# A fifth PSUM bank, decay rows stored by chunk, and decay factors by eight exponentials in the state-space stage of a two-block network

## The chip, the cores and the metric

The kernel runs on one core of one Trainium2 chip. The metric is the device time of that core in microseconds, the median of several executions. Everything is computed in float32; matrix products split each operand into a high part that TensorE takes in one pass and a low rest, and add three products.

## The reference

The reference is a network of two blocks over a sequence of 1024 tokens with 1024 features. The change touches one mixer of the second block, a Mamba-2 layer with 32 heads of width 64 in 4 groups of 8 heads, with a state of 128 per group, computed in 8 chunks of 128 tokens:

```
acum  = cumsum(dt * A)                       # within a chunk, per head
decay = exp(where(t >= s, acum[t] - acum[s], -inf))
y     = (C B^T * decay) @ (x * dt)  +  (C @ state) * exp(acum)
state = state * exp(acum[end])      +  B^T @ (x * dt * exp(acum[end] - acum))
y     = (y + D * x) * silu(z)
y     = rmsnorm over each group's 512 channels
out   = y @ w_out
```

Before that, `z`, `x`, `B` and `C` come from a projection of the normed input, and `x`, `B` and `C` go through a causal convolution of four taps and a silu. The rest of the network (gated spatial mixing, dilated attention, stick-breaking attention, two layers of per-layer embedding) is untouched.

## The kernel before

The activations are kept transposed: a tile holds 128 features on the partitions and 1024 tokens along the free dimension. All weight tiles (128x1024, 512 KB) lie in one array in the order of use. SP loads each into one of two raw buffers, ScalarE makes its high part (L114), and VectorE or GpSimd makes the low part (L119). A raw buffer is free for the tile after next when the low part is made; this is what SP waits for before each load.

`stage_dt` (L1177) computes the step sizes and the running sums: `acum` holds them by token (128 partitions, a column for each chunk and head), and `rows` by head. SP writes `rows` to memory as `acum_dram`, 32 heads by 1024 tokens.

`stage_ssm` (L1326) is a loop over the four groups of heads. In each group TensorE works in this order:

- six convolution tiles (two of B and C, four of x), each a dense product of 48 matmuls, half of them for each 512 columns, into the two banks of `D`;
- four z tiles, cut into 64 units of three matmuls. The first 20 units run alone, then come ten slots, in which units are mixed with the chunk work: `products(c)` (L1436 C times state, L1439 the state's increment, L1442 eight weighted products), `turn_out(c)` (L1450, transposes of y), `turn_in(c)` (L1429 to L1431, transposes of x and B, and the product C B). A slot holds `products` of one chunk, `turn_out` of the chunk before and `turn_in` of the chunk after next;
- sixteen output products of twelve matmuls each (eight row tiles, two halves), which use four banks in turn, number o in bank o % 4. The first four run over three of the four y tiles while the fourth is being made; then the sums of squares (L193), the root on ScalarE, the reciprocal on VectorE, the spread to all columns (L211), and VectorE's copy of it. Only then can VectorE scale an output product and add it to `f_sb` (L1717, L1720), and product o starts when the evacuation of product o - 4 has read its bank.

For each chunk the decay factors are made in `E`, two buffers of 128x1024 in `K.sq` (eight heads by 128 tokens). SP broadcasts the eight head rows to all partitions (L1391), GpSimd subtracts the token's own sum (L1743) and fills the upper triangle with -1e30 (L1746), ScalarE takes the exponential (L1546), and VectorE multiplies by C B (L1607), which releases L1442. A row for chunk c is issued when the products of chunk c - 2 are done. VectorE's other chunk work is x_dt and x_dte (L1599, L1601), the new state (L1615), the sum of y (L1619, L1622), the skip term (L1629), and the evacuation of z units (L1593).

SP's queue holds the loads of the group's weight tiles and the rows in a fixed order: `load(m)` waits for the low part of tile m of the group and fetches tile m + 2. Tiles 0 to 5 are the convolution's, 6 to 9 z's, 10 to 13 the output's. The order is `load(0)` to `load(5)`, rows 0 and 1, `load(6)`, rows 2 and 3, `load(7)`, and so on to `load(9)`, then `load(10)` to `load(13)`. Row 0 waits for the end of the last convolution.

Of the kernel before, what the change touches and what calls it, by code (L numbers as in the profile page):

```python
# [6 lines left out]
F32 = mybir.dt.float32  # L7
F32R = mybir.dt.float32r
ALU = mybir.AluOpType
ACT = mybir.ActivationFunctionType  # L10

P = 128
S = 1024
# [1163 lines left out]
def stage_dt(K, x_sb, f_sb, xhi, xlo, dt, dte, acum, e_acum, e_end, acum_dram):  # L1177
# [5 lines left out]
    with ExitStack() as ctx:  # L1183
# [23 lines left out]
        with nc.Block() as block:  # L1207
            @block.sync
            def _(sp):
                sp.dma_start(raw[:, :, :], io["w_dt"][:, :, :]).then_inc(landed, 16)  # L1210
                sp.dma_start(head[:, :, :], io["dt_head"][:, :].partition_broadcast(P)).then_inc(landed, 16)
                sp.dma_start(tri[:, :], io["causal"][:, :]).then_inc(landed, 16)
                sp.wait_ge(copied, 2)
                sp.dma_start(acum_dram, rows[:, :]).then_inc(stored, 16)
                sp.wait_ge(stored, 16)

            @block.tensor
# [56 lines left out]
            @block.vector  # L1274
            def _(dve):
                dve.wait_ge(h_done, 1)
                dve.tensor_tensor(lo[:, :, :], raw[:, :, :], hi[:, :, :].bitcast(F32), ALU.subtract).then_inc(l_done, 1)
                K.norm_recip(dve, root_done, rtok_done)
                K.norm_copy(dve, spread, spread_done, r_done)
                for k in range(KT + 1):  # L1280
                    if k < KT:
                        dve.scalar_tensor_tensor(f_sb[:, k, :], x_sb[:, k, :], K.gain("g_final", k), K.R[:, :],
                                                 ALU.mult, ALU.mult).then_inc(f_done, 1)
                    if k >= 1:
                        dve.wait_ge(f_done, k)
                        K.tile_lo(dve, xlo, xhi, f_sb, k - 1, "m_norm", x_hi, x_lo)
                dve.wait_ge(f_done, KT)
                K.norm_recip(dve, root2, rtok2)
                steps = [0]

                def step(ins):

                    steps[0] += 1
                    ins.then_inc(v_step, 1)
                    dve.wait_ge(v_step, steps[0])

                dve.wait_ge(t_step, 1)
                step(dve.tensor_tensor(by_head(v[:, :]), by_head(pN[:, 0:W]),
                                       K.rtok[:, :].unsqueeze(2).to_broadcast([P, NC, SH]), ALU.mult))
                dve.wait_ge(landed, 48)  # L1300
                step(dve.tensor_tensor(by_head(v[:, :]), by_head(v[:, :]), all_blocks(head[:, 0, :]), ALU.add))
                K.norm_copy(dve, spread, spread2, r2)


                dve.wait_ge(a_step, 4)
                step(dve.tensor_scalar(d[:, :], e[:, :], 1.0, None, ALU.add))
                step(dve.tensor_scalar(d[:, :], d[:, :], -1.0, 1e-30, ALU.add, ALU.add))
                step(dve.reciprocal(r[:, :], d[:, :]))
                step(dve.scalar_tensor_tensor(l[:, :], l[:, :], 1e-30, r[:, :], ALU.add, ALU.mult))
                step(dve.tensor_tensor(l[:, :], l[:, :], e[:, :], ALU.mult))  # L1310
                step(dve.scalar_tensor_tensor(dt[:, :], v[:, :], 0.0, l[:, :], ALU.max, ALU.add))
                step(dve.scalar_tensor_tensor(by_head(dA[:, :]), by_head(dt[:, :]), -1.0, all_blocks(expA[:, :]),
                                              ALU.mult, ALU.mult))
                dve.wait_ge(t_step, 3)
                step(dve.tensor_copy(acum[:, :], pA[:, 0:W]))
                step(dve.tensor_tensor(dte[:, :], pA[:, W:2 * W], acum[:, :], ALU.subtract))
                dve.tensor_copy(end[:, :], pA[:, W:2 * W]).then_inc(v_step, 1)
                dve.wait_ge(a_step, 6)
                dve.tensor_tensor(dte[:, :], dte[:, :], dt[:, :], ALU.mult)

            @block.gpsimd
            def _(pool):
# [3 lines left out]
def stage_ssm(K, xhi, xlo, f_sb, dt, dte, acum, e_acum, e_end, acum_dram):  # L1326
# [4 lines left out]
    with ExitStack() as ctx:  # L1331
# [5 lines left out]
        pY = ctx.enter_context(nc.psum_tensor("ssm_pY", [P, S], F32))  # L1337
        pS = ctx.enter_context(nc.psum_tensor("ssm_pS", [P, H], F32))
        pT = ctx.enter_context(nc.psum_tensor("ssm_pT", [P, H], F32))
        banks = [D[:, 0:H], D[:, H:S], pX[:, :], pT[:, :]]  # L1340
        BC = sb("BC", [P, 2, S])
        xs = sb("xs", [P, GT, S])
        with ExitStack() as shared:
# [14 lines left out]
        dn, evac = sem("dn"), sem("evac")  # L1358
        cv_a, cv_d, cv_s = sem("cv_a"), sem("cv_d"), sem("cv_s")
        row_land = [sem("row0"), sem("row1")]  # L1360
        seg, sel, ex, weighted, select_go = sem("seg"), sem("sel"), sem("ex"), sem("weighted"), sem("select_go")
        s1, ps_done, s2, s3, cb_copy, xd = sem("s1"), sem("ps"), sem("s2"), sem("s3"), sem("cb_copy"), sem("xd")
        y_inter, y_done, st_decay, st_done, y_turned = sem("y_inter"), sem("y_done"), sem("st_decay"), sem("st_done"), sem("y_turned")
        yz_early, y_hi_early, high_go = sem("yz_early"), sem("y_hi_early"), sem("high_go")
# [10 lines left out]
        with nc.Block() as block:  # L1375
            @block.sync
            def _(sp):
                def group(g):
                    def load(m):

                        n = GROUP_TILES * g + (n0 + m)
                        sp.wait_ge(K.w_lo, n + 1)
                        K.load_weight(sp, n + 2, m % 2)

                    def row(c):

                        if c == 0:
                            sp.wait_ge(cv_d, 18 * g + 18)
                        if c >= 2:
                            sp.wait_ge(s2, 8 * g + (c - 1))  # L1390
                        sp.dma_start(E[c % 2], acum_dram[bass.ds(8 * g, GH), c * P:c * P + P]  # L1391
                                     .partition_broadcast(P)).then_inc(row_land[c % 2], 16)

                    for m in range(6):
                        load(m)
                    for c in range(NC):
                        row(c)
                        if c % 2 == 1:
                            load(6 + c // 2)
                    for m in range(10, 14):  # L1400
                        load(m)

                with sp.Fori(0, GROUPS) as g:
                    group(g)

            @block.tensor
            def _(pe):
# [45 lines left out]
                def group(g):  # L1453
# [20 lines left out]

                    def out_products(o, k):
                        j, half = o // 2, o % 2
                        return K.products(pe, banks[o % 4], j // 2 % 2, 4 * (j % 2) + k, k, yhi, ylo, half,
                                          k == 0, k == GT - 1)


# [10 lines left out]
                    pe.wait_ge(y_lo, 4 * g + 4)  # L1491
                    for o in range(4):
                        out_products(o, GT - 1).then_inc(dn, 1)
                    pe.wait_ge(acc_done, 3 * g + 3)
                    K.norm_sums(pe, pCB, sums_done)
                    K.norm_spread(pe, pY, rtok_done, g + 1, spread_done)
                    for o in range(4, 2 * KT):
                        if o % 4 == 0:
                            pe.wait_ge(K.w_lo, GROUP_TILES * g + (n0 + 11 + o // 4))
                        pe.wait_ge(evac, OUTS * g + (20 + o - 1))  # L1500
                        for k in range(GT):
                            last = out_products(o, k)
                        last.then_inc(dn, 1)
# [5 lines left out]
            def _(act):  # L1509
# [9 lines left out]
                def group(g):  # L1519
# [17 lines left out]
                    for slot in range(10):  # L1537
                        if slot < 8:
                            c = slot
                            act.wait_ge(s1, 8 * g + (c + 1))  # L1540
                            if c >= 2:
                                act.wait_ge(s2, 8 * g + (c - 1))
                            act.activation(cb[:, c % 2, :, :], pCB[:, 0:2 * P].rearrange("p (a b) -> p a b", a=2),
                                           ACT.Copy).then_inc(cb_copy, 1)
                            act.wait_ge(sel, 8 * g + (c + 1))
                            act.activation(E[c % 2], E[c % 2], ACT.Exp).then_inc(ex, 1)  # L1546
                        q_old, q = q, q + sum(Z_UNITS[slot])
                        if q // 16 > q_old // 16:
                            silu_z(q // 16 - 1)
# [35 lines left out]
            def _(dve):  # L1585
# [48 lines left out]
                def group(g):  # L1634
# [78 lines left out]
                    for j in range(KT):  # L1713
                        for half in range(2):
                            cols = slice(half * H, half * H + H)
                            dve.wait_ge(dn, OUTS * g + (20 + 2 * j + half + 1))
                            dve.tensor_tensor(tmp[:, cols], banks[(2 * j + half) % 4], Rg[:, cols],  # L1717
                                              ALU.mult).then_inc(evac, 1)
                            dve.wait_ge(evac, OUTS * g + (20 + 2 * j + half + 3))
                            dve.tensor_tensor(f_sb[:, j, cols], f_sb[:, j, cols], tmp[:, cols], ALU.add).then_inc(scaled, 1)  # L1720
# [11 lines left out]
            def _(pool):  # L1732
                def group(g):
                    for c in range(NC):
# [5 lines left out]
                        for b in ([0, 1] if c == 0 else [c + 1] if c + 1 < NC else []):  # L1740

                            pool.wait_ge(row_land[b % 2], 64 * g + (16 * (b // 2) + 16))
                            pool.tensor_tensor(E[b % 2], E[b % 2], heads(acum, b, g, P), ALU.subtract).then_inc(seg, 1)  # L1743
                            pool.wait_ge(seg, 8 * g + (b + 1))
                            pool.sem_inc(select_go, 1)
                            pool.affine_select(out=E[b % 2], in_=E[b % 2], compare_op=ALU.is_ge, fill=NEG, base=0,  # L1746
                                               pattern=[[0, GH], [1, P]], channel_multiplier=-1).then_inc(sel, 1)
# [787 lines left out]
def bass_program(nc, io, out):  # L2535
    with ExitStack() as ctx:
# [5 lines left out]
        branch_a = nc.dram_tensor("branch_a", (KT, P, S), F32, kind="Internal").ap()  # L2542
        y_dram = nc.dram_tensor("y_b", (KT, P, S), F32, kind="Internal").ap()
        f_dram = nc.dram_tensor("f_copy", (P, KT, S), F32, kind="Internal").ap()
        acum_dram = nc.dram_tensor("acum_rows", (SH, S), F32, kind="Internal").ap()
        x_dram = io["xT"].rearrange("(k p) t -> p k t", p=P)

        ctx.callback(K.clear_semaphores)
# [114 lines left out]
```

## Time and profile before

| | |
|---|---|
| median of 3 runs | 3521.37 us (3518.78 to 3530.22) |
| the profiled execution | 3521.37 us |
| its span, first to last instruction | 3519.9 us |
| TensorE busy | 3181.3 us, 90% of the span |
| VectorE, ScalarE, GpSimd busy | 1852.6, 1359.8, 725.3 us |
| mean granted TensorE clock | 0.946 |
| the state-space stage | from 1486 to 2400 us of the span |

An engine's busy time says how long its instructions ran, not that they were needed at that moment. A row of the timeline has the start, the duration, the engine, the line, the operation with the tiles that it writes and reads, and in brackets the idle time before it with the engine and line that ended it. A granted clock of 1.00 is 2.4 GHz and 0.50 is 1.2 GHz.

### The profile page before, as it was taken

To read this page: it belongs to the slowest core of one execution; us is meant where nothing else is said; L and a number is where in the kernel's file an instruction comes from. 1 tells how busy PE (TensorE), PEld (TensorE's weight loads), DVE (VectorE), ACT (ScalarE), POOL (GpSimd) and SP (SyncE) were. 2 spreads that over 40 slices of the span, in tenths; PEclk is the share of its full clock that TensorE was granted. 3 is DMA by queue.
4 is the path that set the end of the run, shared out by engine and by line. 5 is a ranking of instruction groups with operands and counts; after the bars stand their busy time and mean duration, and the time that the engine had idled before them with its cause. 6 is when DMAs were issued, how large, how long until landed. Compare 5 with 4: busy or idle time off the path is not lost. (4 is left out here: it accounts for less than half of the span.)

```text
span 3519.9 us, 41749 instructions
## 1 busy us (share of the span) xinstructions
PE 3181.3 (90%) x15532; PEld 2634.1 (75%) x15532; DVE 1852.6 (53%) x2499; ACT 1359.8 (39%) x1876; POOL 725.3 (21%) x488
## 2 busy tenths in 40 slices
PE   7999999999997999588988989988889999998799
PEld 5788878888885777476766857767768888887677
DVE  4344215666665322556556555576346776766433
ACT  4333114555554312333222222233236666666331
POOL 2110002222221001202021030120224444443110
PEclk8999999999999999699999989999989999998899
DMA  2111221211211212012121131121111111111211
GB/s 93 44 49 44 77 78 54 61 55 55 67 55 42 102 66 96 21 42 66 42 52 51 42 73 35 48 56 60 61 54 37 37 37 37 37 41 44 108 66 60
DMA packets 83049, 197.35 MB, mean 56 GB/s; under 512 B 6304, under 2 KB 41760, under 8 KB 82624
## 3 DMA queue, kind: packets, MB, share of 16 engines
q1 hardware_dynamic: 74048, 164.66, 15.2%
q0 software_dynamic: 8832, 30.41, 2.8%
q8 instruction: 109, 1.79, 0.2%
q14 instruction: 60, 0.49, 0.0%
HBM read 165.56 MB, written 21.10 MB: 53 GB/s over the span
## 5 line engine op out<-in xcount | busy, mean ns | idle before, releaser
L114 ACT ACTIVATE whi<-wraw 128x1024 fp32r<-128x1024 f32 x208 | 218.4, 1051 | 501.0 <-PE ssm_pT L127 142.7
L119 DVE TENSOR_TENSOR wlo<-wraw,whi 128x1024 fp32r<-128x1024 f32 x176 | 252.0, 1432 | 237.1 <-ACT whi L114 233.8
L125 PE MATMUL ssm_D<-x1hi,whi 128*128 128x512 f32 x640 | 263.0, 411 | 4.4 <-DVEq L1725 4.4
L125 PE MATMUL b_D<-x1hi,whi 128*128 128x512 f32 x640 | 255.0, 398 | 8.0 <-DVEq L999 6.6
L126 PE MATMUL ssm_D<-x1lo,whi 128*128 128x512 f32 x640 | 254.8, 398 | 0.0
L127 PE MATMUL ssm_D<-x1hi,wlo 128*128 128x512 f32 x640 | 254.7, 398 | 0.0
L126 PE MATMUL b_D<-x1lo,whi 128*128 128x512 f32 x640 | 250.7, 392 | 0.0
L127 PE MATMUL b_D<-x1hi,wlo 128*128 128x512 f32 x640 | 250.6, 392 | 0.0
L2156 DVE TENSOR_TENSOR_SCAN stick_keep<-stick_keep 128x896 f32<-128x896 f32 (+7 forms) x128 | 210.6, 1650 | 37.4 <-ACT stick_keep L2071 36.2
L125 PE MATMUL stick_D<-x1hi,whi 128*128 128x512 f32 x512 | 213.7, 417 | 7.4 <-DVE x1lo L152 7.4
L2299 POOL TENSOR_TENSOR stick_rows<-stick_rows,stick_keep 128x896 f32<-128x896 f32 (+7 forms) x128 | 156.9, 1228 | 296.0 <-DVE stick_keep L2156 293.6
L127 PE MATMUL stick_D<-x1hi,wlo 128*128 128x512 f32 x512 | 205.6, 402 | 0.0
L126 PE MATMUL stick_D<-x1lo,whi 128*128 128x512 f32 x512 | 205.0, 400 | 0.0
L844 ACT ACTIVATE att_rows<-att_rows,att_stat 128x896 f32<-128x896 f32 (+7 forms) x128 | 99.5, 778 | 176.0 <-DVE att_stat L935 175.8
L1737 POOL TENSOR_TENSOR ssm_decayed<-ssm_state,heads_e_end 128x512 f32<-128x512 f32 x32 | 33.4, 1043 | 588.3 <-DVE ssm_state L1661 536.5
L119 POOL TENSOR_TENSOR wlo<-wraw,whi 128x1024 fp32r<-128x1024 f32 x32 | 76.6, 2393 | 378.6 <-ACT whi L114 378.6
L125 PE MATMUL a_D<-x1hi,whi 128*128 128x512 f32 x384 | 150.9, 393 | 1.5 <-DVEq L468 1.5
L126 PE MATMUL a_D<-x1lo,whi 128*128 128x512 f32 x384 | 150.0, 391 | 0.0
L127 PE MATMUL a_D<-x1hi,wlo 128*128 128x512 f32 x384 | 150.0, 391 | 0.0
L125 PEld LDWEIGHTS ssm_D<-x1hi,whi 128*128 128x128 f32 x640 | 124.0, 194 | 28.5 <-DVEq L1725 4.8
L127 PEld LDWEIGHTS ssm_D<-x1hi,wlo 128*128 128x128 f32 x640 | 123.5, 193 | 27.0
L125 PEld LDWEIGHTS b_D<-x1hi,whi 128*128 128x128 f32 x640 | 121.0, 189 | 30.3 <-issue 7.0
(385 smaller groups left out, 8099.7 us busy)
## 6 DMA issues: line engine op xcount, KB each, us to landing
wraw<-w_dram SPq DMA_DIRECT2D x208, 512.0 KB, 3.5
sq<-acum_rows SPq DMA_DIRECT2D x32, 512.0 KB, 8.7
att_bias<-alibi_dram SPq DMA_DIRECT2D x16, 512.0 KB, 3.5
stack<-stack POOLq DMA_DIRECT2D x32, 256.0 KB, 3.6
x_sb<-xT_dram SPq DMA_DIRECT2D x8, 512.0 KB, 8.0
branch_a<-sq POOLq DMA_DIRECT2D x8, 512.0 KB, 3.5
y_b<-att_y POOLq DMA_DIRECT2D x8, 512.0 KB, 3.0
f<-y_b SPq DMA_DIRECT2D x2, 2048.0 KB, 8.8
```

Of the source, the lines that this page charges most:

```text
L114: act.activation(self.whi[:, s, :, :], self.wraw[:, s, :, :], ACT.Copy).then_inc(self.w_hi, 1)
L119: dve.tensor_tensor(self.wlo[:, s, :, :], self.wraw[:, s, :, :], self.whi[:, s, :, :].bitcast(F32), ALU.subtract).then_inc(self.w_lo, 1)
L125: pe.matmul(out, self.whi[:, s, w0, :], xhi[:, k, cols], start=start, stop=False)
L126: pe.matmul(out, self.whi[:, s, w0, :], xlo[:, k, cols], start=False, stop=False)
L127: return pe.matmul(out, self.wlo[:, s, w0, :], xhi[:, k, cols], start=False, stop=stop)
L844: act.activation(row, row, ACT.Exp, scale=-1.0, bias=stat[:, r:r + 1], accum_out=rsum[:, r:r + 1]).then_inc(ex, 1)
L1737: pool.tensor_tensor(decayed[:, :].rearrange("p (h d) -> p h d", h=GH), state[:, :].rearrange("p (h d) -> p h d", h=GH), heads(e_end, c, g ...
L2156: dve.tensor_tensor_scan(k, k, k, 1.0, ALU.mult, ALU.bypass).then_inc(scan, 1)
L2299: pool.tensor_tensor(row, row, keep[:, r % 2, S - n + 1:S + 1], ALU.mult).then_inc(ex, 1)
```

## The change

The store of `rows` and the array in memory are laid out by chunk, so that the eight rows of a group and chunk lie side by side. `acum` is negated at the end of `stage_dt`. GpSimd's subtraction goes; the fill is applied to the rows as they land, and the exponential adds `-acum` as a bias, one instruction per head. The output products get a fifth bank (`pS`): product 4 is computed ahead of the norm's sums, and the others take the banks in the order of `BANK_OF`. `load(6)` and all later loads stand one place earlier in SP's queue.

```diff
@@ stage_dt
-                sp.dma_start(acum_dram, rows[:, :]).then_inc(stored, 16)
+                sp.dma_start(acum_dram.rearrange("c h t -> h c t"),
+                             rows[:, :].rearrange("h (c t) -> h c t", c=NC)).then_inc(stored, 16)
...
                 dve.tensor_tensor(dte[:, :], dte[:, :], dt[:, :], ALU.mult)
+                dve.tensor_scalar(acum[:, :], acum[:, :], -1.0, None, ALU.mult)
@@ stage_ssm
-        banks = [D[:, 0:H], D[:, H:S], pX[:, :], pT[:, :]]
+        spaces = [D[:, 0:H], D[:, H:S], pX[:, :], pT[:, :], pS[:, :]]
+        BANK_OF = (0, 1, 2, 3, 4, 2, 3, 0, 1, 2, 3, 0, 1, 2, 3, 4)
+        banks = [spaces[b] for b in BANK_OF]
+        LAST_USE = [max([e for e in range(o) if BANK_OF[e] == BANK_OF[o]], default=None) for o in range(2 * KT)]
@@ SP
-                        sp.dma_start(E[c % 2], acum_dram[bass.ds(8 * g, GH), c * P:c * P + P]
+                        sp.dma_start(E[c % 2], acum_dram[c, bass.ds(8 * g, GH), :]
                                      .partition_broadcast(P)).then_inc(row_land[c % 2], 16)
-                    for m in range(6):
+                    for m in range(7):
                         load(m)
                     for c in range(NC):
                         row(c)
                         if c % 2 == 1:
-                            load(6 + c // 2)
-                    for m in range(10, 14):
+                            load(7 + c // 2)
+                    for m in range(11, 14):
                         load(m)
@@ TensorE
                     for o in range(4):
                         out_products(o, GT - 1).then_inc(dn, 1)
+                    pe.wait_ge(K.w_lo, GROUP_TILES * g + (n0 + 12))
+                    pe.wait_ge(st_done, 9 * g + 9)
+                    for k in range(GT):
+                        last = out_products(4, k)
+                    last.then_inc(dn, 1)
                     pe.wait_ge(acc_done, 3 * g + 3)
                     K.norm_sums(pe, pCB, sums_done)
                     K.norm_spread(pe, pY, rtok_done, g + 1, spread_done)
-                    for o in range(4, 2 * KT):
+                    for o in range(5, 2 * KT):
...
-                        pe.wait_ge(evac, OUTS * g + (20 + o - 1))
+                        pe.wait_ge(evac, OUTS * g + (20 + LAST_USE[o] + 3))
@@ ScalarE
-                            act.activation(E[c % 2], E[c % 2], ACT.Exp).then_inc(ex, 1)
+                            for h in range(GH):
+                                last = act.activation(E[c % 2][:, h, :], E[c % 2][:, h, :], ACT.Exp,
+                                                      bias=acum[:, bass.ds(8 * g + (c * SH + h), 1)])
+                            last.then_inc(ex, 1)
@@ VectorE
-                            dve.tensor_tensor(tmp[:, cols], banks[(2 * j + half) % 4], Rg[:, cols],
+                            dve.tensor_tensor(tmp[:, cols], banks[2 * j + half], Rg[:, cols],
@@ GpSimd
-                            pool.tensor_tensor(E[b % 2], E[b % 2], heads(acum, b, g, P), ALU.subtract).then_inc(seg, 1)
-                            pool.wait_ge(seg, 8 * g + (b + 1))
```

## Rows read from the trace of the kernel before

**Rows 1.** The page's first line

```profile
span 3519.9 us, 41749 instructions
```

**Rows 2.** Waits of TensorE, 1486 to 2400 us: total us, times, longest

```profile
PE ssm_pX L1429 <- DVE acc L1601: 35.0, 4, 9.4
PE ssm_pT L1450 <- DVE ssm_xs L1629: 20.1, 12, 2.8
PE ssm_pY L1436 <- DVE ssm_y_sb L1622: 12.4, 22, 1.8
PE ssm_D L125 <- DVE sq L1717: 8.8, 4, 2.2
PE ssm_pY L1442 <- DVE sq L1607: 7.9, 7, 1.8
```

**Rows 3.** Timeline of the first group, 1550 to 1581 us

```profile
1550.19 1.23 DVE L119 TENSOR_TENSOR wlo<-wraw,whi 128x1024 fp32r<-128x1024 f32 x1
...
1561.11 1.01 SPq L1391 DMA_DIRECT2D sq<-acum_rows  x2
1562.31 4.20 SPq L98 DMA_DIRECT2D wraw<-w_dram  x1
...
1566.04 1.06 ACT L1532 ACTIVATE ssm_z<-ssm_z 128x1024 f32<-128x1024 f32 x1 [4.02 <-DVE ssm_z L1593]
...
1576.86 1.06 ACT L114 ACTIVATE whi<-wraw 128x1024 fp32r<-128x1024 f32 x1 [9.75 <-DMA wraw<-w_dram]
...
1577.95 1.23 DVE L119 TENSOR_TENSOR wlo<-wraw,whi 128x1024 fp32r<-128x1024 f32 x1 [11.94 <-ACT whi L114]
...
1580.43 1.11 PE L1429 MATMUL ssm_pX<-ident,ssm_xs 128*128 128x128 f32 x4 [8.90 <-DVE acc L1601]
```

**Rows 4.** DMA issues of the page: count, KB each, us to landing

```profile
wraw<-w_dram SPq DMA_DIRECT2D x208, 512.0 KB, 3.5
sq<-acum_rows SPq DMA_DIRECT2D x32, 512.0 KB, 8.7
```

**Rows 5.** Windows behind the four head waits, then sum over four third-slot dips

```profile
1580.40:1583.70 3.30, 3.27 (x11) 2.87 (x12) 3.02 (x4) 1.48 (x3) 0.00 (x0) 0.53 0.00 0
...
sum 17.70, PE 17.66 PEld 13.18 DVE 11.99 ACT 5.56 POOL 0.00; mean PE 4.41 PEld 3.30 DVE 3.00 ACT 1.39 POOL 0.00
...
sum 13.60, PE 12.88 PEld 9.89 DVE 11.96 ACT 7.02 POOL 5.10; mean PE 3.22 PEld 2.47 DVE 2.99 ACT 1.75 POOL 1.28
```

**Rows 6.** Timeline of GpSimd, third block of the first group

```profile
1596.44 1.90 POOL L1743 TENSOR_TENSOR sq<-sq,heads_acum 128x1024 f32<-128x1024 f32 x1 [9.23 <-DMA sq<-acum_rows]
1598.57 1.09 POOL L1746 TENSOR_SCALAR_AFFINE_SELECT sq<-sq 128x1024 f32<-128x1024 f32 x1 [0.23 <-POOL sq L1743]
```

**Rows 7.** Timeline of ScalarE in a later stage, two short activations

```profile
2636.70 0.37 ACT L2071 ACTIVATE stick_keep<-stick_scores,stick_q_neg 128x128 f32<-128x128 f32 x1 [0.95 <-PE stick_scores L1921]
2636.97 0.36 ACT L2073 ACTIVATE stick_rows<-stick_scores,stick_q_pos 128x128 f32<-128x128 f32 x1
```

**Rows 8.** Timeline of TensorE and VectorE, norm and outputs of the first group

```profile
1672.57 1.22 DVE L1706 TENSOR_TENSOR acc<-acc,sq 128x1024 f32<-128x1024 f32 x1
...
1675.57 1.84 PE L193 MATMUL ssm_pCB<-ones,acc 128*128 128x1 f32 x16
...
1680.54 0.69 DVE L1717 TENSOR_TENSOR sq<-ssm_D,acc 128x512 f32<-128x512 f32 x1
...
1681.29 0.80 PE L125 MATMUL ssm_D<-ssm_yhi,whi 128*128 128x512 f32 x1 [2.20 <-DVE sq L1717]
...
1683.32 0.69 DVE L1717 TENSOR_TENSOR sq<-ssm_pX,acc 128x512 f32<-128x512 f32 x1
...
1700.10 0.69 DVE L1717 TENSOR_TENSOR sq<-ssm_D,acc 128x512 f32<-128x512 f32 x1 [1.23 <-PE ssm_D L127]
...
1705.54 0.69 DVE L1717 TENSOR_TENSOR sq<-ssm_pT,acc 128x512 f32<-128x512 f32 x1 [1.23 <-PE ssm_pT L127]
```

**Rows 9.** Timeline of VectorE, end of the stage that makes the running sums

```profile
1484.27 0.43 DVE L1319 TENSOR_TENSOR heads_dte<-heads_dte,heads_dt 128x256 f32<-128x256 f32 x1 [0.60 <-ACT heads_dte L1270]
```

More of the change, by code:

```diff
@@ L1360, in stage_ssm @@
         row_land = [sem("row0"), sem("row1")]
-        seg, sel, ex, weighted, select_go = sem("seg"), sem("sel"), sem("ex"), sem("weighted"), sem("select_go")
+        sel, ex, weighted, select_go = sem("sel"), sem("ex"), sem("weighted"), sem("select_go")
         s1, ps_done, s2, s3, cb_copy, xd = sem("s1"), sem("ps"), sem("s2"), sem("s3"), sem("cb_copy"), sem("xd")
@@ L1476, in out_products @@
                         j, half = o // 2, o % 2
-                        return K.products(pe, banks[o % 4], j // 2 % 2, 4 * (j % 2) + k, k, yhi, ylo, half,
+                        return K.products(pe, banks[o], j // 2 % 2, 4 * (j % 2) + k, k, yhi, ylo, half,
                                           k == 0, k == GT - 1)
@@ L2544, in bass_program @@
         f_dram = nc.dram_tensor("f_copy", (P, KT, S), F32, kind="Internal").ap()
-        acum_dram = nc.dram_tensor("acum_rows", (SH, S), F32, kind="Internal").ap()
+        acum_dram = nc.dram_tensor("acum_rows", (NC, SH, P), F32, kind="Internal").ap()
         x_dram = io["xT"].rearrange("(k p) t -> p k t", p=P)
```

## The prediction

> **What bounds the kernel now.** I read the page first, then the waits of TensorE in the stage that the diff touches, then the timeline of each engine around the longest of these waits. The span is 3519.9 us, and the profiled execution took 3521.37 us, which is also the median of the three runs, so the sum below is made against 3521.4 [rows 1]. TensorE is busy for 90% of the span: what shortens the kernel is time in which it waits or in which it runs at the lower clock. In the stretch of the state-space stage (1486 to 2400 us) it waits most in five places [rows 2]: 35.0 us in 4 waits before the second turn-in (L1429), 20.1 us in 12 before turn-outs (L1450), 12.4 us in 22 before the state product (L1436), 8.8 us in 4 before an output product (L125, for the evacuation at L1717), and 7.9 us in 7 before the weighted products (L1442). There are four groups, so the first is nearly 9 us per group.
>
> **The 9 us wait at the head of a group** [rows 3]. SP issues the two row transfers at 1561.11 and only then, at 1562.31, weight tile 8. Its high part is made at 1576.86, when the tile has landed; ScalarE had been free since 1567. VectorE stands in its low split (start 1577.95) with x_dt queued behind, and TensorE waits for x_dt until 1580.43. The chain is thus: rows ahead on the queue, tile 8 late, ScalarE, VectorE, TensorE. In the new order `load(6)` stands ahead of `row(0)`. It waits for tile 6's low split (1550.19, 1.23 us long), so it is issued near 1551.5 and, at the 3.5 us of a lone weight transfer [rows 4], lies ready before 1556. What is late next: silu of z ends at 1567.1, the high part would end at 1568.1, and from the low split's start to TensorE's it is 2.5 us (1577.95 to 1580.43): 1570.6. TensorE arrives at 1580.43 - 8.90 = 1571.5. All 35.0 us go, with 0.9 us to spare. Moved with it: the transfers of tiles 9, 10 and 11 each pass two rows as well, and `row(0)` is not held, since it waits for the convolutions in any case, later than `load(6)`.
>
> **The clock behind that wait.** After each of the four waits the granted clock shows 0.53 or 0.52, the 1.2 GHz level, while TensorE is fully busy, for 17.7 us in all [rows 5]. At 2.4 GHz that work takes half: 8.9 us come back. Each group also has a low stretch of 3.4 us after the waits of its third slot, 12.9 us of work in all, worth up to 6.4 us [rows 5]. Some waits stay there, so I take half, 3.2 us.
>
> **The rows.** Both transfers are 512 KB, but the weight's lands in 3.5 us and the row's in 8.7 us [rows 4]. The diff makes eight 512-byte pieces per partition one contiguous 4 KB piece, the form of the weight tile, so I take 3.5 to 4 us; the bounds are 3.5 and, if nothing changes, 8.7. The trace has no broadcast of one 4 KB piece of this size, so the upper bound isn't firm.
> The Trainium skill ("DMA: Bandwidth & Descriptors", Specifications) gives 512 bytes as the smallest transfer that reaches line rate, and by it the old rows were already at full speed and the new layout would bring nothing. The two rows of this trace, same bytes and 3.5 against 8.7 us, speak against it for this pattern; it is the second rival below.
>
> **Decay factors.** GpSimd's subtraction goes: in the third block it starts at 1596.44 and the selection only at 1598.57, so 2.13 us go from the path [rows 6]. ScalarE's one exponential of 1.06 us becomes eight of 128x128 with a pointer bias. The nearest row is a pair of 128x128 activations with a pointer scale: 0.37 us each, 0.27 us start to start [rows 7]. Eight take 7 x 0.27 + 0.37 = 2.26 us, 1.2 more than now; the bounds are 8 x 0.37 = 3.0 and the 1.06 of now. From row issue to weighted factors it is 5.0 - 1.2 + 2.1 = 5.9 us sooner. The longest of the waits before L1442 is 1.8 us, so all 7.9 us go, also if the exponentials take 3.0. Behind the exponentials on ScalarE stand the silu, the high split and the next cb copy. They start sooner too, since the exponential is done long before the z unit that silu needs. The work added on ScalarE is 32 x 1.2 = 38 us beside idle time, and 62 us of subtraction goes from GpSimd, which decides nothing here.
> The following waits shrink only in part: L1450 waits for the skip operation, which is behind the low split of tile 9, and that needs silu and high part (2.1 us in a row) after the z unit. In the third slot a turn-out that waits now still waits about 0.5 us and the turn-in behind it 0.8. I take 2.3 us there in all groups together and 1.0 us for the later turn-outs, 3.3 of 20.1. The 12.4 us at L1436 (0.28 in most slots, 1.8 before the last block) hang on VectorE's own order and stay.
>
> **The fifth bank** is where I expect a loss. Output product 4 is put ahead of the norm's sums. The sums start at 1675.57 straight after the matmuls before them; the sum they need was ready at 1672.57 + 1.22 = 1673.8 [rows 8]. No idle time is there to fill. Output products take 2.72 us each (1700.10 to 1705.54 for two), so the whole norm chain (sums, root, spread, copy to R) starts 2.72 us later. Behind the copy, TensorE used to start product 4 after the first evacuation (1681.29, the first one starts at 1680.54). Now product 5 lies in bank 2 and waits for the third evacuation, which starts at 1683.32: 2.78 us later. Product 4 is gone from behind, minus 2.72. Per group: 2.72 + 2.78 - 2.72 = 2.8 us longer, 11.1 us in all. Bounds: the wait grows at best from 2.2 to 2.2, if product 4 filled the whole time, -2.7 a group (-11 in all); at worst TensorE is at the low clock for 3.4 us longer, +1.7 a group (+18).
>
> **Edges.** The write of the rows to memory becomes 256 pieces of 512 bytes, and VectorE gets one 128x256 negation behind L1319 (start 1484.27, the stage's last) [rows 9]. VectorE's operations of this size show 0.43 us at most, so I add 0.4 us once; between 0 and 3 if the write takes about as long as a lone weight transfer, and the stage's end waits for it.
>
> **Sum.** 35.0 + 8.9 + 3.2 + 7.9 + 3.3 = 58.3 gained, 11.1 + 0.4 = 11.5 lost: 46.8 us less than 3521.4, that is 3474.6 us. Everything sits in the stage's 914 us; all other stages keep their times.
>
> **Rivals.**
> 1. The fifth bank costs nothing or gains: the profile after would show product 4 inside idle time. For it: TensorE idles 2.2 us before the evacuation now. Against: product 4 is not put into that gap but ahead of the chain that makes it. Time 3474.6 - 11.1 = 3463.5, chance 8%.
> 2. The rows do not land faster (8.7 us stays). Then only 2.13 - 1.2 = 0.9 us per block is gained on that path, about 2.4 of the 7.9 us stay, the follow-up waits (3.3) and the clock's 3.2 stay as well: 3474.6 + 8.9, 3483.5. Chance 8%.
> 3. The lost clock does not come back, or the head of a group finds a new wait of 2 to 4 us (TensorE reaches the turn-in with 0.9 us to spare): 3474.6 + 8.9 + 8 = 3491.5. Chance 8%.
> 4. Slower than before: 128 partitions that read one and the same 4 KB contend in memory, and a row takes 12 us or more. Two buffers alternate, so block c's row is asked for when block c-2 is done. Today's path from there is 8.7 + 2.1 + 1.1 + 1.1 + 1.2 = 14.2 us to the weighted factors, and it misses TensorE by 1.8 at most: 12.4 are free. The new path is the row and 1.1 + 2.3 + 1.2 = 4.6, so rows of up to 7.8 us cost nothing; beyond, each microsecond delays the two chains of blocks, 3 blocks deep each, by about 3 us a group, 12 in all. The gain of 47 is used up at about 12 us, and at 13 the kernel takes some 3536. Against it: the same 4 KB are read 128 times already now. Chance 4%.
>
> The forecast itself has 72%, with a range of its own of 3466 to 3484. The range for 8 in 10 takes in rivals 1 and 2 and much of 3: 3462 to 3490. About 0.3% (10 us) is what a measurement of this kernel tells from no change. Faster by more than that holds in the forecast and in rivals 1 to 3: 0.96; within 0.3%: 0.01; slower: 0.03, these two from rival 4.
>
> **What the profile after would show.** The 35.0 us before the turn-in L1429 gone, and the low clock behind it; if a wait is left there, the first step is wrong. Row transfers near 3.5 us and 32 x (1024 - 128), some 28,000, packets fewer. No TENSOR_TENSOR on sq by GpSimd in this stage, 256 exponentials 0.27 us apart, hardly a wait before L1442. In the tail: the sums start 2.7 us after product 4 instead of at once, and the wait for an evacuation in front of the output products is about 4.9 us instead of 2.2 in each group; if it is below 2.5, the loss was mis-sized. The prediction would be wrong outright if a new wait of several microseconds stood in each group in front of the weighted products.

## The result

The changed kernel takes 3466.32 us (median of 4 runs, 3455.91 to 3470.76) against 3522.03 us before (4 runs), a ratio of 0.9834 with a 95% interval of 0.9806 to 0.9862. The forecast was 3474.6 us with a range of 3462 to 3490; the median lies 8.3 us below it, at the lower edge of the 3466 to 3484 us that the forecast gave itself. The profiled execution took 3455.91 us, 10 us less than the median, while the one of the kernel before (3521.37 us) lay at its median. So the two profiles differ by 65.5 us and the medians by 55.7, and what is read from one profile is compared with the other profile only.

The page of the changed kernel: the span (65.6 us less than in [rows 1]), the packets, and the two kinds of transfers (count, KB each, us to landing).

```profile
span 3454.3 us, 42110 instructions
...
DMA packets 54602, 197.36 MB, mean 57 GB/s; under 512 B 6304, under 2 KB 9248, under 8 KB 54176
...
wraw<-w_dram SPq DMA_DIRECT2D x208, 512.0 KB, 3.5
sq<-acum_rows SPq DMA_DIRECT2D x32, 512.0 KB, 3.7
```

The rows land in 3.7 us instead of 8.7 [rows 4], in the same bytes.

TensorE's waits in the state-space stage, in the same view as [rows 2]:

```profile
PE ssm_pX L125 <- DVE sq L1730: 19.9, 4, 5.0
PE ssm_pT L1455 <- DVE ssm_xs L1642: 13.7, 12, 2.1
PE ssm_pY L1441 <- DVE ssm_y_sb L1635: 13.1, 24, 1.8
PE ssm_D L125 <- DVE ssm_ylo L1670: 7.6, 4, 2.2
PE ssm_D L125 <- DVEq L1738: 4.4, 1, 4.4
PE ssm_pY L211 <- DVE rtok L1721: 2.4, 4, 0.6
PE ssm_pX L1434 <- DVE ssm_scratch L1614: 1.9, 4, 0.5
```

Two of the five waits of [rows 2] are gone, the 35.0 us before the turn-in and the 7.9 us before the weighted products. The turn-outs wait 6.4 us less. One has grown: 19.9 us for an evacuation (now with `pX`, product 5) where there were 8.8. All of the list sums to 63.0 us. The same list of the kernel before holds four more rows than [rows 2] shows (5.2, 4.4, 2.4 and 1.4 us) and sums to 97.6.

The head of the first group, answering to [rows 3]:

```profile
1550.81 0.33 SPq L98 DMA_DIRECT2D wraw<-w_dram  x1
...
1560.33 0.85 SPq L1396 DMA_DIRECT2D sq<-acum_rows  x2
1561.67 0.33 SPq L98 DMA_DIRECT2D wraw<-w_dram  x1
...
1565.26 1.06 ACT L1542 ACTIVATE ssm_z<-ssm_z 128x1024 f32<-128x1024 f32 x1 [4.01 <-DVE ssm_z L1606]
...
1566.23 1.04 ACT L114 ACTIVATE whi<-wraw 128x1024 fp32r<-128x1024 f32 x1
...
1567.30 1.23 DVE L119 TENSOR_TENSOR wlo<-wraw,whi 128x1024 fp32r<-128x1024 f32 x1 [2.07 <-ACT whi L114]
...
1569.05 0.68 DVE L1614 TENSOR_TENSOR acc<-ssm_pX,heads_dte 128x512 f32<-128x512 f32 x1
...
1570.59 0.60 PE L1434 MATMUL ssm_pX<-ident,ssm_xs 128*128 128x128 f32 x4
```

Tile 8 is asked for 9.5 us before the rows, and its high part follows the silu without a gap. VectorE is done with the first chunk at 1569.73, and TensorE starts its second turn-in at 1570.59 without a wait: 0.86 us to spare, where the forecast had 0.9.

The tail of the first group, answering to [rows 8]:

```profile
1655.29 1.22 DVE L1719 TENSOR_TENSOR acc<-acc,sq 128x1024 f32<-128x1024 f32 x1
...
1661.05 1.84 PE L193 MATMUL ssm_pCB<-ones,acc 128*128 128x1 f32 x16
...
1666.02 0.69 DVE L1730 TENSOR_TENSOR sq<-ssm_D,acc 128x512 f32<-128x512 f32 x1
...
1668.80 0.69 DVE L1730 TENSOR_TENSOR sq<-ssm_pX,acc 128x512 f32<-128x512 f32 x1
...
1669.55 0.79 PE L125 MATMUL ssm_pX<-ssm_yhi,whi 128*128 128x512 f32 x1 [4.98 <-DVE sq L1730]
```

The sum of squares is ready at 1656.5, and the norm's sums start at 1661.05, 4.5 us later; before it was 1.8 us. Product 5 starts behind the third evacuation and not the first.

Now the clock. These are windows over the stretches with a granted clock of 0.50 (window and its length, busy time of PE, PEld, DVE, ACT, POOL, clock, DMA share, GB/s), first of the kernel before: the six of the nineteen that lie behind the waits of the seventh and later slots, and the sum over all nineteen.

```profile
1873.70:1877.10 3.40, 3.40 (x4) 1.43 (x5) 3.14 (x7) 0.10 (x1) 0.02 (x1) 0.50 0.00 0
1883.90:1887.30 3.40, 3.40 (x11) 2.82 (x10) 3.40 (x7) 0.00 (x0) 0.00 (x0) 0.50 0.02 5
...
2102.40:2112.60 10.20, 9.41 (x26) 6.81 (x27) 6.19 (x10) 3.32 (x4) 0.58 (x1) 0.50 0.00 0
2116.00:2119.40 3.40, 3.35 (x10) 2.89 (x11) 3.40 (x7) 0.00 (x0) 0.00 (x0) 0.50 0.02 5
...
2334.50:2337.90 3.40, 3.40 (x5) 1.34 (x6) 3.37 (x7) 0.09 (x1) 0.00 (x0) 0.50 0.00 0
2344.70:2348.10 3.40, 3.40 (x12) 2.72 (x10) 3.38 (x7) 0.00 (x0) 0.00 (x0) 0.50 0.02 5
...
sum 112.20, PE 79.85 PEld 59.38 DVE 83.78 ACT 30.50 POOL 15.23; mean PE 4.20 PEld 3.13 DVE 4.41 ACT 1.61 POOL 0.80
```

And all of the changed kernel:

```profile
1483.80:1490.60 6.80, 4.90 (x12) 3.84 (x13) 0.00 (x0) 0.00 (x0) 0.00 (x0) 0.50 0.46 154
1664.70:1674.90 10.20, 5.36 (x13) 4.20 (x14) 8.98 (x12) 0.00 (x0) 0.00 (x0) 0.50 0.11 20
1852.40:1855.90 3.50, 3.50 (x12) 2.76 (x11) 3.47 (x8) 0.00 (x0) 0.00 (x0) 0.51 0.02 5
1879.70:1886.60 6.90, 2.94 (x7) 2.36 (x8) 6.61 (x10) 0.00 (x0) 0.00 (x0) 0.51 0.01 2
2091.40:2101.60 10.20, 5.34 (x13) 4.18 (x14) 8.99 (x12) 0.00 (x0) 0.00 (x0) 0.50 0.08 18
2306.40:2316.70 10.30, 5.71 (x13) 4.46 (x14) 8.91 (x13) 0.00 (x0) 0.00 (x0) 0.50 0.13 40
sum 47.90, PE 27.75 PEld 21.80 DVE 36.95 ACT 0.00 POOL 0.00; mean PE 4.62 PEld 3.63 DVE 6.16 ACT 0.00 POOL 0.00
```

TensorE worked 79.9 us at 1.2 GHz before and 27.8 after; half of the difference, 26.1 us, is what the clock gave back in these two executions. With that the stage is accounted for: from its first matmul to the first of the next stage it was 924.6 us and is 863.7, 60.9 less, of which 34.6 are waits (97.6 to 63.0) and 26.1 clock. The other 4.6 us between the two profiles lie outside the stage; behind it, TensorE's busy time is 4.4 us shorter for the same instructions (999.96 and 995.52 us), which is clock too.

The other three executions of the changed kernel show a granted clock of 0.951 to 0.953 against 0.955 in the profiled one. Only the profiled one has a trace. If the waits of the others sum to 63.0 us as well, the clock gave back 55.7 - 34.6 = 21.1 us between the medians; this is an estimate.

### The profile page after: what moved, and what is told of

Its sections match the earlier page's. It is cut to its first block and busy times, and to the rows that moved or that the text cites. A ratio compares the mean times of both kernels' runs of the same rounds, so it can differ in the third digit from the quotient of the medians.

```text
span 3454.3 us, 42110 instructions
## 1 busy us (share of the span) xinstructions
PE 3150.5 (91%) x15532; PEld 2613.9 (76%) x15532; DVE 1853.2 (54%) x2500; ACT 1404.7 (41%) x2100; POOL 673.3 (19%) x456
```

## The experiments

For each profile the stage splits in the same way. "Waits" is the sum of TensorE's waits in the stage, "rest" the stage less the waits. (The sum takes in the wait before the stage's first matmul, 4.2 to 4.6 us, and leaves out the one before the next stage's first, 5.5 us, so each rest holds about 1 us of idle time.) The rest less half of TensorE's busy time at the low clock is 785 to 788 us in all 14 profiles: that is the work at 2.4 GHz, 786 us in what follows, and what exceeds it is the price of the low clock. The ratio is that of timed runs to the kernel before on the same chip, and the difference is (ratio - 1) x 3522 us. Stage, waits and rest are of the profiled execution alone; the last column says by how much it was longer than the median of its kernel. A difference of some microseconds between two rests can be that alone.

| kernel | ratio (95%) | difference | stage | waits | rest | profiled less median |
|---|---|---|---|---|---|---|
| before | 1 | 0 | 924.6 | 97.6 | 827.0 | -1 |
| changed | 0.9834 (0.9806 to 0.9862) | -58 | 863.7 | 63.0 | 800.7 | -10 |
| changed again (e9) | 0.9833 (0.9815 to 0.9851) | -59 | 864.2 | 63.8 | 800.4 | -11 |
| e1 four banks in changed | 0.9798 (0.9776 to 0.9820) | -71 | 858.1 | 50.7 | 807.4 | +5 |
| e2 early load only | 0.9894 (0.9872 to 0.9916) | -37 | 883.2 | 62.9 | 820.3 | -4 |
| e3 rows by chunk only | 0.9854 (0.9832 to 0.9875) | -51 | 866.5 | 62.0 | 804.5 | -7 |
| e4 fifth bank only | 1.0040 (1.0024 to 1.0055) | +14 | 940.6 | 111.1 | 829.5 | +9 |
| e5 decay factors only | 0.9973 (0.9958 to 0.9988) | -10 | 920.6 | 97.7 | 822.9 | -3 |
| e6 old rows in changed | 0.9876 (0.9855 to 0.9897) | -44 | 893.4 | 72.8 | 820.6 | +2 |
| e7 banks in rotation | 0.9799 (0.9777 to 0.9821) | -71 | 859.6 | 51.0 | 808.6 | 0 |
| e8 product 4 behind spread | 0.9760 (0.9739 to 0.9781) | -85 | 841.3 | 43.8 | 797.5 | -2 |
| e10 e8, old queue | 0.9750 (0.9729 to 0.9771) | -88 | 845.7 | 43.3 | 802.4 | +7 |
| e11 e8, subtraction back | 0.9789 (0.9767 to 0.9812) | -74 | 859.7 | 51.3 | 808.4 | +5 |
| e12 sixteen exponentials | 0.9876 (0.9855 to 0.9898) | -44 | 883.2 | 63.9 | 819.3 | 0 |

**e1, the fifth bank undone in the changed kernel.**

```diff
-        BANK_OF = (0, 1, 2, 3, 4, 2, 3, 0, 1, 2, 3, 0, 1, 2, 3, 4)
...
+        banks = [D[:, 0:H], D[:, H:S], pX[:, :], pT[:, :]]
...
-                        return K.products(pe, banks[o], j // 2 % 2, 4 * (j % 2) + k, k, yhi, ylo, half,
+                        return K.products(pe, banks[o % 4], j // 2 % 2, 4 * (j % 2) + k, k, yhi, ylo, half,
...
-                    for k in range(GT):
-                        last = out_products(4, k)
-                    last.then_inc(dn, 1)
...
-                    for o in range(5, 2 * KT):
+                    for o in range(4, 2 * KT):
```

> The changed kernel with the fifth bank undone: four banks in turn, product 4 behind the norm again, all else as changed. Theory A (the fifth bank is a loss, because product 4 stands ahead of the chain that makes the idle time): the waits for an evacuation in front of the output products fall from 19.9 to 8.8 us in all, and the kernel is 11 us faster than the changed one, 3455 us against 3466. Theory B (product 4 fills idle time elsewhere, the waits only move): the same time as the changed one within 3 us, with waits of the same sum in other places of the tail.

It is 3450.2 us, a ratio of 0.9798 against 0.9834. The wait for the evacuation, the same view as above:

```profile
PE ssm_D L125 <- DVE sq L1722: 8.8, 4, 2.2
```

Theory A holds: 8.8 us, and some 12 us less than the changed kernel by the ratios. The intervals of the two overlap a little; the waits (63.0 to 50.7) don't depend on them.

**e2, only the queue's order changed** (`range(7)`, `load(7 + c // 2)`, `range(11, 14)`).

> The kernel before with one part of the change: load(6) and all later loads one place earlier in SP's queue. Theory A (tile 8 is late because the two rows stand ahead of it): the four waits in front of the turn-in (35.0 us) go, and the low clock behind them (8.9 us): 44 us faster than before, 3478 us. The waits before the weighted products stay or grow, since the rows still take 8.7 us. Theory B (what matters is that the rows themselves are slow): less than 15 us gained, the wait comes back in the first products of a group.

3483.79 us, 37 us gained. The head waits are gone, as A has it, and the other waits stay (22.5 us before turn-outs, 6.7 before the weighted products). The clock paid less than assumed: the rest fell by 6.7 us, not 8.9 (in one profile each).

**e3, only the rows by chunk.**

> The kernel before with one part of the change: the rows stored by chunk, so that a transfer has 4 KB pieces. Theory A (order of the queue decides): tile 8 still stands behind two rows, so a wait is left at the head of each group. Worked out from the transfers: two rows of 2.4 us each and then tile 8 land near 1569 instead of 1576.9, so TensorE waits about 1 us instead of 8.9: 31 us gained there, 8 us of clock, and 7.9 + 3.3 us in front of the weighted products and turn-outs: 3472 us. Theory B (order alone decides, the layout only helps the later blocks): about 12 us gained, 3510 us.

3467.83 us, 51 us gained, more than e2. Theory B falls, and the transfer times decide: two fast rows delay tile 8 so little that the head wait all but goes without any change of order. The waits:

```profile
PE ssm_pY L1443 <- DVE sq L1608: 5.8, 9, 0.8
PE ssm_D L125 <- DVEq L1726: 4.4, 1, 4.4
PE ssm_pX L1430 <- DVE acc L1602: 4.1, 4, 1.1
```

4.1 us at the heads instead of 35.0 [rows 2]. My A expected the waits before the weighted products to go too; 5.8 of 7.9 us stay (see e11).

**e4, only the fifth bank.**

> The kernel before with one part of the change: the fifth bank with BANK_OF, product 4 ahead of the norm's sums. Theory A: 11 us slower than before (3533 us), the wait for an evacuation in front of the output products 19.9 us instead of 8.8. Theory B: no change within 3 us.

3537.56 us, 0.4% slower, with the interval above 1. The wait:

```profile
PE ssm_pX L125 <- DVE sq L1725: 19.9, 4, 5.0
```

A holds, in the place and size forecast.

**e5, only the decay factors.**

```diff
-                            act.activation(E[c % 2], E[c % 2], ACT.Exp).then_inc(ex, 1)
+                            for h in range(GH):
+                                last = act.activation(E[c % 2][:, h, :], E[c % 2][:, h, :], ACT.Exp,
+                                                      bias=acum[:, bass.ds(8 * g + (c * SH + h), 1)])
+                            last.then_inc(ex, 1)
...
-                            pool.tensor_tensor(E[b % 2], E[b % 2], heads(acum, b, g, P), ALU.subtract).then_inc(seg, 1)
-                            pool.wait_ge(seg, 8 * g + (b + 1))
```

> The kernel before with one part of the change: no subtraction on GpSimd, eight exponentials per block with -acum as bias; rows and queue as before. Theory A: the path from a row to its weighted factors is 2.1 - 1.2 = 0.9 us shorter, so the 7.9 us of waits before the weighted products fall to about 2.4 and the rest of the stage stays, the head waits of 35 us too: 5 to 8 us faster than before, 3515 us. Theory B (eight short instructions hold ScalarE up): no gain or a loss of some us, with longer waits for the high part of a weight tile or for cb.

3517.37 us against 3528.35 us before on the same chip, a ratio of 0.9973: about 10 us gained. The size is near A, its mechanism isn't: the waits before the weighted products are 6.7 us and not 2.4, and all waits sum to 97.7, as before. In the third block of the four groups the wait was 1.80, 1.77, 1.57 and 0.95 us and is 0.93, 1.63, 0.95 and 0.66, so the 0.9 us of the shorter path show in full in the first group only; one wait in the last block of the first group grew from 0.80 to 1.94. The profile shows 4 us in the rest. What the gain hangs on stays open here.

**e6, the rows by head again in the changed kernel.**

> The changed kernel with the rows stored by head again (512-byte pieces, 1024 packets a row), all else as changed. Theory A (the rival 2 of the prediction, worked out): the head waits stay away, since load(6) is ahead of the rows; rows take 8.7 us again and some 2 us of waits per group come back in front of the weighted products and turn-outs, with some clock: 6 to 10 us slower than the changed kernel, 3474 us. Theory B: the layout is worth much more, over 20 us, because a row with small pieces also delays the tiles behind it in the queue.

3482.41 us, a ratio of 0.9876, 15 us slower than the changed kernel: between the theories. The head waits stay away; 7.4 us before the weighted products come back, where the forecast's second rival had 2.4, and the turn-outs wait 20.6 us again instead of 13.7. The waits grow by 9.8 us. Between the two profiles the rest grows by 20 us, but the changed kernel's profile was 10 us faster than its median and this one 2 us slower: of the 15 us between the timed runs only about 5 are left for the clock.

**e7, the fifth bank in rotation.**

```diff
-        BANK_OF = (0, 1, 2, 3, 4, 2, 3, 0, 1, 2, 3, 0, 1, 2, 3, 4)
+        BANK_OF = (0, 1, 2, 3, 4, 0, 1, 2, 3, 4, 0, 1, 2, 3, 4, 2)
```

> The changed kernel with another BANK_OF only: (0,1,2,3,4,0,1,2,3,4,0,1,2,3,4,2). Product 4 stays ahead of the norm's sums, but product 5 now lies in bank 0 and waits for the first evacuation, not the third. Theory A: of the loss of 2.8 us a group all goes, since it is 2.78 us from the first to the third evacuation: 11 us faster than the changed kernel, equal to four banks. Theory B (the delay of the norm chain by product 4 is what costs): nothing gained.

A ratio of 0.9799, equal to four banks (0.9798), and the wait for the evacuation is 8.8 us again. So the whole loss is the choice of bank 2 for product 5 (`BANK_OF` differs in later places too, but this wait is the one that moved), and putting product 4 ahead of the norm alone neither gains nor loses.

**e8, product 4 behind the spread, banks as in e7.**

```diff
                     for o in range(4):
                         out_products(o, GT - 1).then_inc(dn, 1)
+                    pe.wait_ge(acc_done, 3 * g + 3)
+                    K.norm_sums(pe, pCB, sums_done)
+                    K.norm_spread(pe, pY, rtok_done, g + 1, spread_done)
                     pe.wait_ge(K.w_lo, GROUP_TILES * g + (n0 + 12))
...
                     last.then_inc(dn, 1)
-                    pe.wait_ge(acc_done, 3 * g + 3)
-                    K.norm_sums(pe, pCB, sums_done)
-                    K.norm_spread(pe, pY, rtok_done, g + 1, spread_done)
```

> The changed kernel with the rotated banks of e7, and product 4 moved from ahead of the norm's sums to behind the spread, where TensorE waits 2.2 us for VectorE's copy and first evacuation in the kernel before. Theory A: product 4 (2.7 us) covers that wait whole, so the norm chain is as early as with four banks and the wait before an output product is near 0: 11 + 8.8 = 20 us faster than the changed kernel, plus what the clock gives back, 3446 us or less, the best of all. Theory B: it equals e7, because VectorE's evacuations are then late for products 5 and 6.

3442.77 us, a ratio of 0.976, the best form with the change's own parts, 26 us better than the changed kernel by the ratios. TensorE's and VectorE's timelines in the first group:

```profile
1672.95 1.09 PE L211 MATMUL ssm_pY<-ident,rtok 128*128 128x128 f32 x8 [0.59 <-DVE rtok L1721]
1673.80 0.48 PE L125 MATMUL ssm_pS<-ssm_yhi,whi 128*128 128x512 f32 x1
...
1675.49 0.69 DVE L1730 TENSOR_TENSOR sq<-ssm_D,acc 128x512 f32<-128x512 f32 x1
...
1676.65 0.39 PE L125 MATMUL ssm_D<-ssm_yhi,whi 128*128 128x512 f32 x1
```

Product 4 (`pS`) fills 1673.8 to 1676.6, in which VectorE copies the spread and makes the first evacuation (ready at 1676.2); product 5 follows without a wait.

**e9, the changed kernel once more.**

> The changed kernel itself once more, to read how its low-clock stretches vary and to have it beside e10 to e12. Theory A (the clock is what the prediction mis-sized): in the state-space stage the length is 786 us plus TensorE's waits plus half of its busy time at the low clock, as in the profiles so far (before 97.6 and 81.6, changed 63.0 and 28.5). The waits come out at 63 us again; the busy time at the low clock may lie between 25 and 50 us. Theory B (the stage's work itself got shorter): the rest would differ from 786 by several us. Time 3466 us, within 10.

3467.58 us. Waits 63.8, rest 800.4: the profile repeats, and Theory A holds (half of 28.1 us of work at the low clock leaves 786.3). Here too the profiled execution is the fastest of its kernel, 9 us ahead of the next. (The 81.6 and 28.5 us of the expectation are read with windows laid a little later than those shown above, which gave 79.9 and 27.8.)

**e10, e8 with the old order of the queue.**

> The best so far (e8: product 4 behind the spread, rotated banks) with load(6) behind rows 0 and 1 again. Theory A (with rows of 3.7 us the order of the queue is nearly redundant): a wait of about 1 us at the head of each group as in e3 (4.1 us in all) and hardly anything else: 3447 to 3452 us against 3443. Theory B (the order of the queue carries the gain at the head): the 35 us of waits come back, 3480 us or more.

A ratio of 0.975 against 0.976: no difference that can be told. A holds; the head waits are 1.9 us in all, where 4.1 were expected. With fast rows the early load is all but redundant: the early load alone removes the 35.0 us of head waits (e2), the fast rows alone all but 4.1 of them (e3).

**e11, e8 with the subtraction on GpSimd and one exponential.**

> e8 with the subtraction on GpSimd and one exponential per block again, rows by chunk, load(6) ahead. Theory A: the path from a row to its factors is 0.9 us longer and the rows leave over 4 us of room, so the waits before the weighted products stay near 0: within 4 us of e8, 3443 to 3447 us, that is, eight exponentials are worth nothing once the rows are fast. Theory B (GpSimd's 62 us contend with VectorE, or e3's 5.8 us of waits before the weighted products come from the subtraction): 6 to 12 us slower than e8, 3450 to 3455 us.

A ratio of 0.9789 against 0.976, 10 us slower (the intervals overlap a little). Theory B's place is right: 6.5 us of waits before the weighted products, in a kernel whose rows are early. Timelines of VectorE, GpSimd and TensorE in one block:

```profile
1621.82 1.90 POOL L1752 TENSOR_TENSOR sq<-sq,heads_acum 128x1024 f32<-128x1024 f32 x1 [2.11 <-DMA sq<-acum_rows]
1621.87 2.92 DVE L1616 TENSOR_TENSOR sq<-sq,ssm_cb 128x1024 f32<-128x1024 f32 x1
...
1624.85 1.33 PE L1446 MATMUL ssm_pY<-ssm_scratch,sq 128*128 128x64 f32 x10 [0.80 <-DVE sq L1616]
```

VectorE's pass over the factors, 1.22 us in the median of the 32, takes 2.92 us while GpSimd's subtraction runs beside it, and TensorE waits 0.80 us for it. In the same trace a pass that starts just ahead of the subtraction keeps its time, and the subtraction is stretched instead:

```profile
1613.86 1.22 DVE L1616 TENSOR_TENSOR sq<-sq,ssm_cb 128x1024 f32<-128x1024 f32 x1
...
1613.88 2.95 POOL L1752 TENSOR_TENSOR sq<-sq,heads_acum 128x1024 f32<-128x1024 f32 x1 [2.13 <-DMA sq<-acum_rows]
```

Ten of the 32 passes start while a subtraction runs, take 2.6 to 2.9 us, and are the ten for which TensorE waits. Before, none of the 32 ran beside one; the fast rows had moved the subtraction into VectorE's pass. In e3 nine passes take 2.6 to 3.0 us beside a subtraction, and TensorE waits for just these nine: its 5.8 us are the same thing. With the subtraction gone the upper-triangle fill still stretches nine passes, to 2.0 to 2.1 us (e8), and TensorE waits for none of them.

**e12, sixteen exponentials in place of eight.**

> The changed kernel with sixteen exponentials of 128x64 per block in place of eight of 128x128, the same work in twice as many instructions. Eight take 2.45 us from first start to last end; sixteen should take some 4 us. Theory A (ScalarE has room there, the split costs nothing): within 5 us of the changed kernel, 3466 to 3471 us. Theory B (ScalarE is near its limit, so the split into eight already costs): 10 us or more slower, with waits before the weighted products.

3486.51 us, a ratio of 0.9876, 15 us slower than the changed kernel. From ScalarE's timeline of the changed kernel, and from ScalarE's and TensorE's of e12:

```profile
1569.72 2.45 ACT L1557 ACTIVATE sq<-sq,heads_acum 128x128 f32<-128x128 f32 x8
```

```profile
1577.24 3.93 ACT L1559 ACTIVATE sq<-sq,heads_acum 128x64 f32<-128x64 f32 x16
...
1582.57 1.66 PE L1447 MATMUL ssm_pY<-acc,sq 128*128 128x64 f32 x13 [1.11 <-DVE sq L1622]
```

The first block of a group has no room: 1.1 us of new wait there, 4.5 in all, given back elsewhere (the sum of waits is 63.9 against 63.0). Neither theory had what happened: the rest grew by 18.6 us. Some 10 of them can be the changed kernel's fast profile; but with waits only 0.9 us longer, most of the 15 us between the timed runs must be the clock's too. In the first group both kernels have the same waits from the seventh slot on (0.93, 1.78 and 2.09 us; 0.93, 1.80 and 2.09 in the changed kernel). In e12 the clock falls within the second of them, which ends at 1638.58, and in the changed kernel it doesn't fall there at all:

```profile
1637.70:1647.90 10.20, 9.32 (x26) 6.80 (x27) 6.26 (x11) 3.51 (x7) 0.64 (x1) 0.50 0.00 1
```

## Why the prediction was right, step by step

- **Head wait, 35.0 us.** Gone, in place and size. Shown by e2. It would have all but gone without the early load as well (e3: 4.1 us left, e10: 1.9): the forecast named the queue's order as its cause, and the cause was that order together with the small pieces of each row, 1024 by the layout where there are now 128 (the forecast had some 28,000 packets fewer; the two pages differ by 28,447). Its own two transfer rows [rows 4] were enough to see it.
- **Clock, 12.1 us.** The term that was mis-sized: 26.1 us in the profiled executions, about 21 between the medians by the estimate above. Of the 26.1, the stretches at the heads gave 8.4 (forecast 8.9), those of the third slots 6.5 (forecast 3.2: I took half, and all of them went), and the late ones 11.4, for which I had put nothing, because the waits before them would stay. For the most part these waits did stay: in groups two to four 1.42, 1.57 and 1.51 us, each followed by 1.80 and 2.09, became 0.93, 0.94 and 1.58, followed by the same 1.80 and 2.09. Yet of the six stretches behind them one was left (1852.4). In group four even the first wait is no shorter, and two stretches became none, so the lengths of these waits don't explain it.
- **Rows.** Forecast 3.5 to 4 us, measured 3.7. The transfer rate of 4 KB pieces against 512-byte pieces of the same bytes is shown by 3.7 against 8.7 us, and by e6 with the layout alone turned back. The rule of the Trainium skill ("DMA: Bandwidth & Descriptors", Specifications) that 512 bytes reach line rate does not hold for this broadcast read; the measurement decides.
- **Decay factors, 7.9 + 3.3 us.** Eight exponentials take 2.45 us (forecast 2.26). The waits before the weighted products went whole, and it takes both parts: 5.8 us stay with fast rows alone (e3), 6.7 with the new factors alone (e5). The turn-outs, 3.3 us, gave 6.4: in the third slots 0.2 us of wait is left in each group where 0.5 were expected. What was not seen is that the subtraction, once the rows are fast, would have run beside VectorE's pass and stretched it (e11).
- **Fifth bank, a loss of 11.1 us.** The wait grew from 8.8 to 19.9 us, 11.1. The forecast added three terms: the later norm (+2.72 us a group), the third evacuation (+2.78), product 4 gone from behind (-2.72). e7 shows that the first and the last cancel and the third evacuation is all of it.
- **Sum.** Waits: 35.1 us forecast (35.0 + 7.9 + 3.3 - 11.1), 34.6 measured. That they agree so closely is in part luck: the turn-outs gave 3.1 us more than forecast, and three other waits, for which no change was forecast, grew by 3.6 (12.4 to 13.1, 5.2 to 7.6, 1.4 to 1.9). Of the 19 us between forecast and the profiled execution, 14.0 are the clock's in this stage and 4.6 lie in the other stages, which were to keep their times. The 8 us between forecast and median are most likely the clock's too; no trace of those executions shows it.
- **Rivals.** 1 (bank free) is refuted by e4 and e1, 2 (rows not faster) and 4 (a row of 12 us) by the landing times. 3 did not come, neither a new wait at the head nor a clock that stays low. The second rival's own price of 8.9 us was too small: with the old layout alone turned back the kernel is 15 us slower than the changed one, and 7.4 us wait before the weighted products, not 2.4 (e6).

## What to carry to other kernels

Before moving a product into a gap, look whether it is put into the gap or ahead of the chain that makes it: here the same product cost nothing ahead of the norm and was worth 14 us behind the spread (e8 against e7), and the bank chosen for one product cost 12 (e7). When a wait hangs on a queue, ask whether its order or the size of its packets is at fault; either cure may do, and the two don't add up. TensorE's waits can be added and subtracted row by row; what the clock adds to them has to be given a range of its own.

## What was not expected of the hardware

- The low clock costs 11 to 44 us in this stage, beside waits of 43 to 111, and follows the waits loosely: the rest lies between 797.5 and 829.5 us for the same work of 786. In e12 the waits grew by 1 us and the rest by 19, and waits of nearly the same lengths went with 9.3 us of work at 1.2 GHz there and with none in the changed kernel. Two profiles of one kernel agree within 1 us (changed and e9), but its other executions were 9 to 15 us longer at a lower mean clock (0.950 to 0.954 against 0.955). What sets it was not found; no run moved the waits in time and left all else.
- GpSimd and VectorE slow each other, and it is the one that starts second that is stretched: a 128x1024 VectorE pass of 1.22 us took 2.92 us when a GpSimd subtraction of the same size had started 0.05 us before it, and the subtraction of 1.90 us took 2.95 when the pass had started 0.02 us before.
- Cutting one exponential of 128x1024 (1.06 us) into eight costs 1.4 us and into sixteen 2.9 us: 0.29 and 0.24 us from one start to the next.
